# Hybrid RWKV-7 / sparse-attention step: the samples' attention becomes a fourth projection stage, each pair's RWKV norm moves into the next pair, and the prompt stage's weight splits move to VectorE

## The reference

```python
xn = rms_norm(x, norm_in)
u  = einsum('btd,dc->btc', xn, w_in)          # 2048 -> 94 chunks of 128 columns here
u_a, u_b, u_m = split(u)                      # RWKV, attention, merge gates

# mixer A, RWKV-7, 16 heads of 64, per token:
sa = einsum('bhij,bhj->bhi', S, kk_t)
S  = S * w_t - sa (kk_t * a_t) + v_t k_t
o  = einsum('bhij,bhj->bhi', S, r_t)
o  = (o - mean) * rsqrt(var + GN_EPS) * gn_w + gn_b     # per head
o  = (o + sum(r * k * r_k) * v) * silu(g)

# mixer B, sparse attention, 16 query heads on 4 key/value heads of 64:
# compressed blocks, the 16 best of 33 blocks of 64 keys, a window of 512 keys
o = g0 * o_cmp + g1 * o_sel + g2 * o_win
o = o * silu(g_b)

h = x + (sig(u_m[0]) * (o_a @ w_pa) + sig(u_m[1]) * (o_b @ w_pb)) @ w_o
```

## Time and profile before

| what | value |
|---|---|
| median of 3 runs | 2625.93 us (2620.84 to 2628.12) |
| the profiled execution's own time | 2622.69 us |
| its span | 2620.5 us |
| PE busy | 2308.7 us (88%) |
| VectorE busy | 1187.0 us (45%) |
| ScalarE busy | 790.7 us (30%) |
| GpSimd busy | 441.7 us (17%) |
| DMA | 301.65 MB, mean 115 GB/s |

### The profile page before, as it was taken

How to read it: one execution, slowest core, us unless ns; L and a number is a source line. 1 busy time by engine, 2 the same in 40 slices (tenths; PEclk the granted TensorE clock), 3 DMA queues, 4 the chain that set the end, 5 groups by cost and what they waited for, 6 DMA issues and landing times. The chain is left out here.

```text
span 2620.5 us, 51046 instructions
## 1 busy us (share of the span) xinstructions
PE 2308.7 (88%) x21174; PEld 2102.2 (80%) x21174; DVE 1187.0 (45%) x2330; ACT 790.7 (30%) x1494; POOL 441.7 (17%) x239
## 2 busy tenths in 40 slices
PE   5999999999999999999999789999246637999996
PEld 4998989898988888899999777888223327999996
DVE  4244545444454545348898144444223425443223
ACT  4343333333332332122222344544111113232111
POOL 0000000000000000001100499999200000000000
PEclk8999999999999999999999899999668877999998
DMA  3321222222221212268775513221575632342232
GB/s 116 98 83 60 83 64 75 64 79 60 80 79 60 80 62 85 75 198 287 226 254 186 153 57 93 69 85 44 164 236 170 189 115 103 124 146 106 102 101 93
DMA packets 124556, 301.65 MB, mean 115 GB/s; under 512 B 24218, under 2 KB 37156, under 8 KB 118596
## 3 DMA queue, kind: packets, MB, share of 16 engines
q1 hardware_dynamic: 97972, 242.44, 29.1%
q0 software_dynamic: 7696, 32.78, 3.6%
q10 hardware_dynamic: 18688, 23.59, 2.8%
HBM read 261.55 MB, written 45.54 MB: 117 GB/s over the span
## 5 line engine op out<-in xcount | busy, mean ns | idle before, releaser
L177 PE MATMUL acc<-xh,w_hi 128*128 128x272 f32 x3008 | 670.5, 304 | 24.0 <-DVE xl L433 12.0
L177 PE MATMUL acc<-xh,w_lo 128*128 128x272 f32 x3008 | 624.8, 289 | 0.0
L177 PE MATMUL acc<-xl,w_hi 128*128 128x272 f32 x3008 | 623.8, 289 | 0.0
L177 PEld LDWEIGHTS acc<-xh,w_hi 128*128 128x128 f32 x3008 | 472.1, 190 | 76.0 <-issue 45.4
L177 PEld LDWEIGHTS acc<-xl,w_hi 128*128 128x128 f32 x3008 | 475.7, 190 | 0.0
L177 PEld LDWEIGHTS acc<-xh,w_lo 128*128 128x128 f32 x3008 | 473.4, 190 | 0.0
L160 DVE TENSOR_TENSOR w_lo<-w_raw,w_hi 128x1024 fp32r<-128x1024 f32 x166 | 203.2, 1224 | 412.6 <-ACT w_hi L152 411.5
L152 ACT ACTIVATE w_hi<-w_raw 128x1024 fp32r<-128x1024 f32 x188 | 198.5, 1056 | 301.1 <-PE acc L177 245.7
L1171 DVE SCALAR_TENSOR_TENSOR b_C<-b_rows,b_pos_s,b_C 128x512 f32<-128x512 f32 x240 | 162.4, 743 | 0.0
L893 PE MATMUL rbank<-m 64*64 64x64 f32 x3840 | 130.9, 220 | 1.1 <-DVE m L584 1.1
L893 PEld LDWEIGHTS rbank<-m 64*64 64x64 f32 x3840 | 118.8, 135 | 15.2 <-issue 3.8
(11 more groups left out here) (386 smaller groups left out, 3350.6 us busy)
## 6 DMA issues: line engine op xcount, KB each, us to landing
w_raw<-in_w_all SPq DMA_DIRECT2D x188, 512.0 KB, 3.6
b_rows<-in_cmp_rows SPq DMA_DIRECT2D x128, 256.0 KB, 3.7
d_kv<-in_sel_kv SPq DMA_DIRECT2D x128, 256.0 KB, 2.9
m_w<-in_w_mo SPq DMA_DIRECT2D x32, 1024.0 KB, 5.7
m_gates<-tmp_uT SPq DMA_DIRECT2D x16, 544.0 KB, 3.7
out_s_win<-in_win_in POOLq DMA_DIRECT2D x8, 1016.0 KB, 5.8
tmp_uT<-ub POOLq DMA_DIRECT2D x24, 272.0 KB, 2.3
tmp_uT<-ub ACTq DMA_DIRECT2D x23, 272.0 KB, 2.6
```

The lines of the kernel that those rows point to most:

```text
L177: ins = self.nc.tensor.matmul(acc[:, c, 0:HALF], w[:, k % KH, :], x[:, k, c * HALF:(c + 1) * HALF], start=(k == 0 and m == 0), stop=(k == ...
```

## The change

**Stages.** Stage 1 has 45 chunks: 9 ahead, 36 pieces per pair; ORDER puts the query chunks there. Stages 2 and 3 keep their 25 and 12 chunks, later ones of the list. `attend_samples` becomes a fourth stage in the same block, with the last 12 chunks woven in: 40 pieces ahead of its 84 jobs and 56 among them, which is two pieces behind every three jobs. One barrier goes, and the drain of GpSimd at the end of a block is left out.

**A pair of stage 1.** `mean`, `S_out`, `var` and the normalization of a pair run inside the next pair's first jobs (`normal_pieces`; its reciprocal in four parts of 128 columns); after the last pair they stand as `END_JOBS`. The state has two tiles, `S[0]` and `S[1]`: a step reads one and writes the other, `S` is issued ahead of `O`, and the first step needs no `U`, since the state is zero. The order and gaps of the other jobs change too; operands of the next pair are prepared in the scan's gaps.

**Stage 3.** The low splits go from GpSimd to VectorE, one behind a unit's maxima; GpSimd runs the RWKV steps alone.

**Stage 4.** Pages are loaded in units: a unit is the window, or four pages of each of two samples (eight transfers of 128 KB), five units a round, once for keys on SP's queue and once for values on GpSimd's, each with a ring of three units. `sel_kv` is split into `sel_k` and `sel_v` to that end. The projection's weights are loaded by ScalarE's queue. A unit's slot is loaded again when the job that read it is done. The exponential is taken per 512 scores. The value products are turned round: 32 rows by 128 columns where it was 64 rows by 256, so that four of them stand in different parts of the array.

The diff, cut to its core:

```diff
-FRONT_CHUNKS, KEY_CHUNKS = 57, 82
+FRONT_CHUNKS, KEY_CHUNKS, PROMPT_CHUNKS = 45, 70, 82
...
-        order += [plain.pop(0) for _ in range(2)]
-        order += PAIR_CHUNKS(i + 2) if i < 6 else [plain.pop(0) for _ in range(4)]
-    return order + KV_CHUNKS + list(range(70, N_CHUNK))
+    others = [c for c in range(33, N_CHUNK) if c not in Q_CHUNKS and c not in KV_CHUNKS]
+    plain = list(Q_CHUNKS) + others[:FRONT_CHUNKS - 33 - len(Q_CHUNKS)]
+    order = [LORA_CHUNK]
+    for p in range(8):
+        if p in (2, 4, 6):
+            order.append(plain.pop(0))
+        order += PAIR_CHUNKS(p)
+    return order + plain + KV_CHUNKS + [c for c in others if c not in order + plain]
 
...
+    ("N", 1, 1, "dve", 1), ("NT", 2, 1, "dve", 0), ("bk_tok0", 0, 1, "act", 1), ("mean", 3, 1, "dve", 0),
+    ("D2", 1, 1, "act", 0), ("DT2", 2, 1, "dve", 0), ("bk_tok1", 0, 1, "act", 1),
     ("G0", 3, 1, "dve", 0), ("G1", 0, 1, "dve", 0),
-    ("D4", 1, 1, "act", 1), ("DT4", 2, 1, "dve", 0),
-    ("G2", 3, 1, "dve", 0), ("G3", 0, 1, "dve", 0),
+    ("D4", 1, 1, "act", 0), ("DT4", 2, 1, "dve", 0), ("var", 3, 1, "act", 1),
+    ("G2", 0, 1, "dve", 0), ("G3", 3, 1, "dve", 0),
...
-SCAN_HEADS = {0: "tok_a", 1: "knorm", 4: "tok_b"}
+SCAN_HEADS = {1: "knorm", 2: "tok_a", 4: "tok_b"}
 NEXT_PAIR = ("tail", "zw", "za", "tok_a", "knorm", "tok_b")
+LAST_PAIR = ("S_out", "mean", "var")
 for _n in range(NCH):
-    PAIR_JOBS += [(f"U{_n}", 1, 1, "dve", 2), (f"O{_n}", 3, 1, "act", 1), (f"S{_n}", 0, 1, "dve", 0)]
+    if _n:
+        PAIR_JOBS.append((f"U{_n}", 1, 1, "dve", 2))
+    PAIR_JOBS += [(f"S{_n}", 0, 1, "dve", 1), (f"O{_n}", 3, 1, "act", 0)]
     if _n in SCAN_HEADS:
         PAIR_JOBS.append((SCAN_HEADS[_n], 2, 1, "dve" if SCAN_HEADS[_n] == "knorm" else "act", 0))
-PAIR_JOBS += [("S_out", 1, 1, "act", 1), ("mean", 2, 1, "dve", 1), ("var", 3, 1, "act", 3)]
+END_JOBS = [("mean", 1, 1, "dve", 1), ("S_out", 0, 1, "act", 1), ("var", 2, 1, "act", 3)]
...
+                        got(f"U{n}")
+                        stt(out=UV[0:CH, n, :].rearrange("p (h i) -> p h i", h=2),
+                            in0=bank[0:CH, bank_of[i, f"U{n}"], 0:P].rearrange("p (h i) -> p h i", h=2), scalar=-1.0,
+                            in1=W2[:, :, n, :], op0=ALU.mult, op1=ALU.subtract).then_inc(ev_dve, 1)
+                        dve.wait_ge(ev_dve, out_at[i, f"S{n - 1}"][1])
+                        link(ts(Sd[:, :], here[:, :], last_p, None, ALU.mult))
+                    else:
+                        background(place[i, "S0"])
+                        taken(dve, (i, "W2a"), (i, "W2b"))
+                        ts(UV[0:CH, n, :].rearrange("p (h i) -> p h i", h=2), W2[:, :, n, :], -1.0, None, ALU.mult)\
+                            .then_inc(first_u, 1)
+                    go_on(preparing, AFTER_U[n])
...
+                    here = S[n % 2]
+                    if n:
+                        job(i, f"U{n}", (i, "W1T"), (i, f"S{n - 1}"))
+                        done(mm(bank[0:CH, bank_of[i, f"U{n}"], 0:P], mats["W1T"][:, n, :], here[:, :],
+                                start=True, stop=True))
+
+                    job(i, f"S{n}", *([(i, f"U{n}")] if n else []), (i, "bk_tok1"))
+                    if n == 0:
+                        pe.wait_ge(first_u, i + 1)
                     for h, hp in enumerate(H):
                         ins = mm(bank[hp, bank_of[i, f"S{n}"], 0:CH], BKtok[:, n, h * CH:(h + 1) * CH],
                                  UV[:, n, h * CH:(h + 1) * CH], start=True, stop=True)
                     done(ins)
+
+                    job(i, f"O{n}")
+                    b = bank_of[i, f"O{n}"]
+                    if n:
+                        mm(bank[:, b, 0:CH], here[:, :], KR[:, n, 1, :], start=True, stop=False)
+                    for h, hp in enumerate(H):
+                        ins = mm(bank[hp, b, 0:CH], UV[:, n, h * CH:(h + 1) * CH],
+                                 G[:, h, n, CH:P], start=(n == 0), stop=True)
+                    done(ins)
...
                 w, t = divmod(u, N_TILE)
                 if u + 1 < NU:
                     maxes(u + 1)
+                background(place["T0", u])
                 dve.wait_ge(exp_done, 2 * u + 2)
...
+N_BP, N_UNIT, N_RING = DEC_B // 2, 5, 3
+SAMPLE_PIECES, SAMPLE_START = PIECES * (N_CHUNK - PROMPT_CHUNKS), 40
...
+    for bp in range(N_BP):
+        for name in ("W", "K0", "sm+", "K1", "K2", "K3", "ptc+", "TW", "imp+", "Tn", "T0", "PW", "imp2+", "T1", "P0",
+                     "T2", "P1", "T3", "P2", "P3", "Pn"):
+            if name[-1] != "+":
+                order.append((name, bp))
+            elif bp + 1 < N_BP:
+                order.append((name[:-1], bp + 1))
...
+        place[job] = SAMPLE_START + (k + 1) * (SAMPLE_PIECES - SAMPLE_START) // len(order)
...
+        def load_unit(eng, u, ring, landed, window, pages):
+
+            bp, n = divmod(u, N_UNIT)
+            for b2 in range(2):
+                b = 2 * bp + b2
+                dst = ring[u % N_RING][:, b2, :, :]
+                if n == 0:
+                    eng.dma_start(*window(dst, b)).then_inc(landed[u % N_RING], 16)
+                    continue
+                for p in range(4):
+                    at = b * N_PAGES + 4 * (n - 1) + p
+                    page = eng.value_load(table[0:1, at:at + 1], min_val=0, max_val=N_POOL - 1)
+                    eng.dma_start(dst[:, p, :], A[pages][bass.ds(page, 1)].rearrange("a p n -> (a p) n"))\
+                        .then_inc(landed[u % N_RING], 16)
...
+            for job in order:
+                if job[0] == "sm" and job[1] + 1 < N_BP:
+                    sp.wait_ge(pe_jobs, done_at[job])
+                    load_kc(job[1] + 1)
+                if job in KEYS and KEYS.index(job) + N_RING < len(KEYS):
+                    sp.wait_ge(pe_jobs, done_at[job])
+                    load_keys(KEYS.index(job) + N_RING)
...
+            for u in range(N_RING):
+                load_unit(pool, u, vU, v_in, window, "sel_v")
+            for u, job in enumerate(VALUES):
+                if u + N_RING < len(VALUES):
+                    pool.wait_ge(pe_jobs, done_at[job])
+                    load_unit(pool, u + N_RING, vU, v_in, window, "sel_v")
...
+                    if at_load <= min(at_high, at_evac):
+                        W.load(act, loads[0])
+                        loads[0] += 1
...
+            def values(b, bp, n):
+                u = N_UNIT * bp + n
+                taken(pe, (("TW", "T0", "T1", "T2", "T3")[n], bp))
+                pe.wait_ge(v_in[u % N_RING], arrivals(u))
+                c0 = P if n == 0 else 0
+                for c in range(4):
...
-            for stage in (rwkv, rest, attend_prompt):
+        with nc.Block(no_gpsimd_drain=True) as block:
+            for stage in (rwkv, rest, attend_prompt, attend_samples):
                 stage(nc, A, T, block)
```

More of the change, by code:

```diff
@@ L867, in _, with bk_turned @@
             for i in range(8):
[L868 removed]
+                background(place[i, "N"])
                 pe.wait_ge(operands, i + 1)
[L870 removed]
+                def bk_turned(name, n0):
                     job(i, name)
@@ L1958, in _ @@
+            background(SAMPLE_PIECES)
+            store(N_BP - 1)
+            act.wait_ge(sent, 16 * N_BP)
+            for j in range(2):
+                act.wait_ge(stored[j], 16 * ((W.s1 - W.s0 + 1 - j) // 2))
+            T.end(act, None, 0)
         @block.vector
```

1051 lines of the change are left out of this document (604 added, 447 removed), and 8 rows, old and new, of the table PAIR_JOBS.

## The result

The changed kernel takes 2608.33 us (median of 4 runs, 2605.63 to 2609.49), the kernel before 2626.04 in the same comparison: ratio 0.9934, 95% interval 0.9917 to 0.9951. It is faster by 17.7 us, 0.7%, where 99 were forecast. The profiled execution has a span of 2606.2 us.

What follows compares the result with a forecast made beforehand. TensorE was taken as the bound, standing still only in the samples' attention, a hole for projection. 2622.7 − 133 + 0 + 6 + 28 = 2524 us, with 3.2 for the median 2527; range 2445 to 2610.

Steps and rivals of the forecast that it cites:

- rival C: Prompt's attention: VectorE's low splits wait for GpSimd's 7 to 9 us instructions; +40, 2567 us in all; chance 0.22.
- B: Stage 1: the chain loses its cover, a pair takes 114.5 us instead of 104, 2611 in all; chance 0.09.
- The price of a chunk: Projection on TensorE: 96 matmuls of 0.124 us each, 12.0 us a chunk, 1.5 a piece.
- Stage 1, −133: Eight pairs: twelve chunks leave (−144), other work rises 1.4 us to 50.0, so a pair takes 104 instead of 120.6.
- queues ahead of UV: Stage 1, VectorE: busy about 53 of 104 us instead of 57 of 120, with queued work before UV; +2 us a pair.
- Stage 3, +6: Prompt's attention: 22 splits of 1.225 us move to VectorE, a third showing, 9 us less some 3; between −5 and +25.
- Stage 4, 318: Samples' attention: projection 144, jobs 68, switches 11, keys 43, values 34, clock 10, ends 8; +28 on 289.7 us.
- The term for the clock: Stage 4: page waits of 8 to 11 us lower TensorE's clock for a few us each; +10 us.
- ScalarE's weight loads: Stage 4: they queue behind ScalarE's exponentials; counted at nothing because two halves lie ahead; a wait there would show the forecast wrong.
- A: Stage 4: the loads keep up at pitches near 0.6 us, the stage takes 231, 2440 in all; chance 0.13.
- D: Stage 4: GpSimd's page loads set the pace; slower from 2.97 us a page, 2664 in all at 3.2; chance 0.03.
- E: Whole kernel: no change that can be told, stage 4 losing what stage 1 gives by B and half of C; chance 0.02.

Runs made afterwards that it cites:

- e8: Changed kernel with VectorE evicting UV ahead of the projection's next low split, at the first and every other scan step of a pair: 2581.17 us, ratio 0.9841.
- e7: Changed kernel with each unit's eight pages loaded half by SyncE's queue and half by GpSimd's, for keys and values: 2553.58 us, ratio 0.9732.
- e3: Changed kernel with GpSimd's samples' RWKV steps left out but for one whole-state product, low splits still on VectorE: 2567.27 us in one run.
- e5: Changed kernel with only the first three units of keys and values loaded, later units computed from what lies in the rings: 2516.84 us in one run.

## Why the prediction was wrong

The direction was right, the size was not: −17.7 us for −99. The result lies just inside the stated range, 2445 to 2610, which had been drawn wide enough for rival C and most of B. By its own steps:

- **The price of a chunk and the second stage** held: the second stage stayed at 323.4, and TensorE's busy time in a pair fell by 15.0 us, from 116.7 to 101.7, for 18.0 of projection; some 2 of the missing 3 are the lower clock (0.98).
- **Stage 1, −133, measured −94.6.** I set +0.5 to 1 us for the first `UV` "straight from W2" and +2 for "queues ahead of UV". The first alone was 22.5/8 = 2.8 us a pair with a stretch at the lower clock behind it. I had counted VectorE's time, which has room (430 of 871 us), and not what its queue's next instruction waits for. For the clock in the pairs the sum has nothing, and the trace shows it at the lower level for 37 us of the stage (before: never). e8 shows that 26.4 of the 38 us are splits in front of `UV`; the other 12 are, by e8's trace, the 3.4 us at the lower clock behind the one wait of 2.1 us that each of seven pairs keeps, and no run takes that wait away. The normalization in the next pair, which I named as the first thing to look at, costs nothing: its reciprocals stand in front of `DiT` and no wait of TensorE for them is in the trace.
- **Stage 3, +6, measured +39.8.** This is the step that failed worst: a split was taken as 1.225 us, and it took 3.7 in the mean. The mechanism stood in the prediction as rival C at +40, with 0.22, and it came as priced: 60 us of waiting where I had estimated 70, and +39.8. That the total agrees so well is in part luck. I had thought of 2 us at each of 20 meetings; 12 us fell at the stage's start, where three splits took 20.55 us (of that stretch I had said that its 18 us remain), 9 are clock, and the same code cost 14 us more in e7's profile. I took the other branch because no row showed it, although the Trainium skill's rule stated it plainly and nothing in the trace spoke against it. The argument for room on VectorE (gaps of 1.5 us in `a_part`) was true, and e3 confirms it; it did not bear on the question.
- **Stage 4, 318, measured 329.7** from the last prompt product (1796.9) to the last stage. The waits were well sized: 39.8 for keys (43) and 30.3 for values (34), pitches 1.05 and 1.15 (1.10 and 1.3). The term for the clock was too small: 10 against 22 by e5. What I had taken for a few us behind each wait is a stretch of 30 us in each round of some 60 with a clock of 0.73. And ScalarE's weight loads, "which I count at nothing", cost TensorE 7.9 us once, the sign that the prediction had named; by the trace the half was late because the DMA engines were full at the stage's start, and no exponential stood ahead of it; no run tries this apart.
- **The last stage** and the barrier: as said.

Together: 38 + 34 + 12 = 84 us lost on the way, against a span that fell by 14.3 instead of 99.

Of the rivals, A (loads keep up) is refuted by the 70 us of waits, and e5 gives its price. B was half true (108.8 us a pair, halfway from 104 to 114.5), with another cause. C holds. D is far: 1.15 us a page against the 2.97 from which it would decide. E, at 0.02, comes nearest to the total, since half of B and the whole of C came together with a stage 4 that was too dear; I had counted them one at a time.

One premise of the prediction is wrong, without harm: it says that no VectorE instruction of the prompt stage read two tiles of SBUF before. The stage's first ones did, but GpSimd stood idle beside them (1468 to 1486), so they could show nothing of C:

```profile
1467.85 0.44 DVE L1367 TENSOR_TENSOR s_kraw<-sx,stab 128x256 f32<-128x256 f32 x1 [6.82 <-DMA stab<-in_stab]
```

Two numbers of the prediction don't follow from its own terms, and neither changes the forecast: with both pitches at 1.8 its waits sum to 395 and not 365 us if none covers another, and C's 2567 adds its +40 on top of the +6 that it replaces (2561).
